# Router products taken from the un-normalised sum in a two-layer decoder trunk

## The reference, cut to what matters

```python
x = layer_norm(DN_ALPHA * x + mix, ln_mix_g[layer], ln_mix_b[layer])
x = layer_norm(DN_ALPHA * x + memory_cross_attention(...), ln_xa_g[layer], ln_xa_b[layer])
x = layer_norm(DN_ALPHA * x + hierarchical_moe(x, ...), ln_ffn_g[layer], ln_ffn_b[layer])

def hierarchical_moe(x, wg, bg, we, be, w1, w3, w2):
    g_logits = xf @ wg + bg                      # 4 groups
    g_star = jnp.argmax(g_logits, axis=-1)
    e_logits = (xf @ we + be)[group g_star]      # 8 experts of the group
    top_val, top_idx = lax.top_k(e_logits, 2)
    ...
    y = (silu(xb @ w1[e]) * (xb @ w3[e])) @ w2[e]   # per expert, weighted and summed
```

## Time and profile before

| what | us |
|---|---|
| median of 3 runs | 1432.13 |
| lowest and highest run | 1429.75, 1433.57 |
| profiled execution, first to last instruction (span) | 1427.2 |
| what the median has beside that span | 4.9 |
| PE busy | 1157.1 (81%) |
| DVE busy | 397.7 (28%) |
| ACT busy | 169.2 (12%) |
| read from memory | 473.62 MB |

### The profile page before, as it was taken

One profiled execution on the slowest core, in us unless ns is written; L12 is line 12 of the kernel. 1 busy time (PEld: TensorE's weight loads), 2 busy tenths in 40 slices (PEclk: granted clock), 3 DMA queues, 4 the chain that ended last, 5 costly groups with the idle time before them and its releaser, 6 DMA issues.

```text
span 1427.2 us, 32903 instructions
## 1 busy us (share of the span) xinstructions
PE 1157.1 (81%) x11774; PEld 723.4 (51%) x11775; DVE 397.7 (28%) x1046; ACT 169.2 (12%) x473; POOL 38.4 (3%) x81
## 2 busy tenths in 40 slices
PE   8999999988797686768789999999987676766665
PEld 7885448554453343334348866655543333333332
DVE  1963532252222121112133123253321111111113
ACT  1202501101110010001010001111110000000001
POOL 4000000001000000000000000000000000000000
PEclk9999999999999898889899999999998888888887
DMA  9756106679999999999995656454999999999994
GB/s 310 269 177 236 60 29 242 266 307 423 429 428 429 428 428 429 428 428 429 428 408 218 236 176 261 163 221 187 410 430 428 428 429 428 429 429 428 428 430 208
DMA packets 64820, 477.34 MB, mean 334 GB/s; under 512 B 4188, under 2 KB 11676, under 8 KB 39948
## 3 DMA queue, kind: packets, MB, share of 16 engines
q1 hardware_dynamic: 62572, 469.97, 80.5%
q0 software_dynamic: 2208, 6.81, 1.5%
HBM read 473.62 MB, written 3.15 MB: 334 GB/s over the span
## 4 chain that ended last, share of the span: by engine, by line
PE 51%; DMA 41%; issue 3%; DVE 2%; ACT 1%; ACTq 1%; SPq 0%; DVEq 0%; POOL 0%
DMA ring<-in_moe_w_dram 41%; PE bank L550 15%; PE bank L959 11%; PE bank L563 8%; PE bank L975 3%; PE bank L744 2%; PE bank L983 2%; PE bank L945 2%; PE bank L520 1%; PE bank L845 1%; PE bank L863 1%; PE bank L902 1%; PE bank L619 1%; PE bank L966 0%; SPq L457 0%
## 5 line engine op out<-in xcount | busy, mean ns | idle before, releaser
L959 PE MATMUL bank<-ring,xT 128*32 128x256 f32 x4672 | 351.0, 466 | 204.4 <-DMA ring<-in_moe_w_dram 200.5
L959 PEld LDWEIGHTS bank<-ring,xT 128*32 128x32 f32 x4672 | 192.3, 133 | 357.9 <-issue 236.1
L550 PE MATMUL bank<-xT,ring 128*128 128x256 f32 x832 | 181.6, 379 | 4.2 <-issue 2.3
L550 PEld LDWEIGHTS bank<-xT,ring 128*128 128x128 f32 x832 | 157.4, 190 | 26.4 <-issue 5.1
L975 PE MATMUL bank<-slot,xT 128*32 128x256 f32 x2336 | 140.1, 380 | 2.7 <-DVE xT L1517 2.5
L1507 DVE SCALAR_TENSOR_TENSOR xT<-xT,bank 64x256 f32<-64x256 f32 x73 | 30.3, 415 | 368.6 <-ACT xT L1750 368.6
L563 PE MATMUL bank<-ring,slot 128*128 128x512 f32 x256 | 111.5, 593 | 4.0 <-ACT slot L1724 2.0
L975 PEld LDWEIGHTS bank<-slot,xT 128*32 128x32 f32 x2336 | 77.4, 110 | 53.9 <-issue 8.7
L983 PE MATMUL bank<-xT 32*128 32x256 f32 x1200 | 85.9, 400 | 19.8 <-issue 18.4
L1493 DVE TENSOR_TENSOR xT<-iota,place 128x64 f32 (+1 forms) x73 | 16.4, 225 | 275.0 <-issue 272.5
L1750 ACT ACTIVATE xT<-bank 64x256 f32<-64x256 f32 x73 | 27.5, 377 | 538.8 <-PE bank L959 520.9
(11 more groups left out here) (273 smaller groups left out, 782.6 us busy)
## 6 DMA issues: line engine op xcount, KB each, us to landing
ring<-in_moe_w_dram SPq DMA_DIRECT2D x126, 2048.0 KB, 33.5
slot<-in_moe_w_dram SPq DMA_DIRECT2D x64, 2048.0 KB, 38.4
ring<-in_od_w_in_dram SPq DMA_DIRECT2D x6, 2048.0 KB, 21.4
ring<-in_xa_wq_dram SPq DMA_DIRECT2D x4, 2048.0 KB, 12.0
ring<-in_xa_wo_dram SPq DMA_DIRECT2D x4, 2048.0 KB, 11.9
ring<-in_ev_w_in_dram SPq DMA_DIRECT2D x3, 2048.0 KB, 14.7
ring<-in_mem_wk_dram SPq DMA_DIRECT2D x2, 2048.0 KB, 15.6
ring<-in_mem_wv_dram SPq DMA_DIRECT2D x2, 2048.0 KB, 12.2
```

The lines of the kernel that those rows point to most:

```text
L550: ins = mm(ps, w[:, k, c0:c0 + P], rhs[:, k, :], start=(k == 4), stop=(k == 3))
L959: ins = mm(b1[qs[2 * m + h], 0:S], xg[:, k, :], ws[m][:, k, h, :, :], start=(k == 0), stop=(k == KC - 1))
```

## The change

In LayerNorm 3L + 1 of both layers, PE no longer waits for the normalised rows. It transposes the sum s = ALPHA * x + f as it stands, and the router's products are taken with s. The logits of LN(s) * gain + bias are

rstd * (s @ (gain * W) - mean * sum(gain * W)) + (bias @ W + router bias),

so W is multiplied by the gain once, at the start of layer 0's mixer projection on DVE (`fold_router`), the sums over features are made by one product with a matrix of ones on PE and taken over by DVE (`take_fold`), and `group_logits` applies mean, rstd and the new bias to 36 columns. The rows of x are made by two instructions of the form (x - mean) * gain and x * rstd + bias (`centred`, `scaled`) where there were three. The transposed rows leave the banks as plain copies. `keep_warm` is gone at this place. Tile 0 and tile 1 are routed one after the other. `start_sum(q, 1)`, q = 1 to 3, is moved behind the hidden layer of the first expert.

```diff
@@ PE
             def normal(i, t):
-                if i % 3 == 2:
+                if i % 3 == 1:
+                    for h in range(2):
+                        wait_drained(pe, ("f", i, t, h))
+                elif i % 3 == 2:
...
             def out_projection(name, i, between=None):
...
                         if t == 1 and h == 0:
                             turned(("n", i), x, 0)
+                            if between is not None:
+                                between()
...
+            def fold_router():
+                ps = claim(pe, ("fold",))
+                pe.wait_ge(wr_folded, 1)
+                n = 2 * DEPTH * (NG + NE)
+                filled(mm(ps[:, 0:n], ones[:, :], scr[:, :, :].rearrange("p a s -> p (a s)")[:, S:S + n], start=True, stop=True), ("fold",))
...
-                out_projection(f"wo_mix{L}", 3 * L)
+                out_projection(f"wo_mix{L}", 3 * L, fold_router if L == 0 else None)
...
-                def logits(t, warm=0):
-                    ps = claim(pe, ("lg", L, t))
-                    keep_warm(ps, warm)
-                    for k in AS_TURNED:
-                        fresh_part(3 * L + 1, k, t)
-                        ins = mm(ps[:, 0:NG + NE], xT[:, k, t * P:(t + 1) * P], wr[:, L, k, :], start=(k == 4), stop=(k == 3))
-                    filled(ins, ("lg", L, t))
-                logits(0)
-                turned(("n", 3 * L + 1), x, 1, 7)
-                logits(1, 6)
+                def logits(t, part):
+                    if part == 0:
+                        claim(pe, ("lg", L, t))
+                        for h in range(2):
+                            wait_drained(pe, (("n", 3 * L + 1), t, h))
+                    ps = banks[bank_of[("lg", L, t)][0]]
+                    for k in range(4 * part, 4 * part + 4):
+                        ins = mm(ps[:, 0:NG + NE], xT[:, k, t * P:(t + 1) * P], wr[:, L, k, :], start=(k == 0), stop=(k == KC - 1))
+                    if part == 1:
+                        filled(ins, ("lg", L, t))
+                if L == 0:
+                    wait_drained(pe, ("fold",))
+                logits(0, 0)
+                turned(("n", 3 * L + 1), x, 1)
+                logits(0, 1)
+                logits(1, 0)
+                logits(1, 1)
...
-                for q in range(1, Q):
-                    start_sum(q, 1)
...
                 unit_hidden(moe_slots[L][0], ready_at(0, 0), 1)
+                for q in range(1, Q):
+                    start_sum(q, 1)
@@ DVE
+        def raw_to_xT(v, i, t):
+            ps = wait_filled(v, (("n", i), t, 1))
+            drained(nc.vector.tensor_copy(xT[:, 4:KC, t * P:(t + 1) * P], ps[:, :].rearrange("p (k s) -> p k s", k=4)), (("n", i), t, 1))
+        def centred(st, v, i, t):
+            v.wait_ge(gb_loaded, 32 * (i + 1))
+            for h in range(2):
+                wait_filled(v, (("n", i), t, h))
+            return st.mark(nc.vector.scalar_tensor_tensor(out=x[:, t, :], in0=x[:, t, :], scalar=mv[:, t, 0:1], in1=gb[:, 0, :],
+                                                          op0=ALU.subtract, op1=ALU.mult))
+        def scaled(st, v, i, t, centred_at):
+            st.wait(centred_at)
+            v.wait_ge(ln_rstd, 2 * i + t + 1)
+            nc.vector.scalar_tensor_tensor(out=x[:, t, :], in0=x[:, t, :], scalar=rstd[:, t, :], in1=gb[:, 1, :],
+                                           op0=ALU.mult, op1=ALU.add).then_inc(x_ready[t], 1)
...
+            def fold_router():
+                v.wait_ge(small_loaded, 16 * 12)
+                flat = scr[:, :, :].rearrange("p a s -> p (a s)")
+                for L in range(DEPTH):
+                    for m in (1, 0):
+                        w = wr[:, L, :, :] if m == 0 else flat[:, 0:KC * NR // 2].rearrange("p (k n) -> p k n", n=NR)
+                        sums = flat[:, S + (2 * L + m) * NR:S + (2 * L + m + 1) * NR]
+                        for half in range(2):
+                            ks = slice(4 * half, 4 * half + 4)
+                            dst = w[:, ks, :] if m == 0 else w
+                            st.do(tt(dst, wr[:, L, ks, :], lngT[:, 3 * L + 1, m, ks].unsqueeze(2).to_broadcast([P, 4, NR]), ALU.mult))
+                            if m == 1:
+                                part = sums if half == 0 else e01[:, :, :, :].rearrange("p t m e -> p (t m e)")[:, 0:NR]
+                                st.do(nc.vector.tensor_reduce(part, w.rearrange("p k n -> p n k"), AX, ALU.add))
+                                if half == 1:
+                                    st.do(tt(sums, sums, part, ALU.add))
+                            elif half == 1:
+                                st.do(nc.vector.tensor_reduce(sums, w.rearrange("p k n -> p n k"), AX, ALU.add))
+            def take_fold():
+                ps = wait_filled(v, ("fold",))
+                v.wait_ge(bias_loaded, 32)
+                for L in range(DEPTH):
+                    ts(wr_sum[:, L, :], ps[:, 2 * L * NR:(2 * L + 1) * NR], -1.0, None, ALU.mult)
+                    ins = tt(rbias[:, L, :], rbias[:, L, :], ps[:, (2 * L + 1) * NR:(2 * L + 2) * NR], ALU.add)
+                drained(ins, ("fold",))
...
                 def group_logits(t):
-                    st.do(tt(g8[:, t, 0:NG], ps[:, 0:NG], rbias[:, L, 0:NG], ALU.add))
-                    drained(tt(lg[:, t, :, :], ps[:, NG:NG + NE].rearrange("p (g e) -> p g e", g=NG),
-                               rbias[:, L, NG:NG + NE].rearrange("p (g e) -> p g e", g=NG), ALU.add), ("lg", L, t))
+                    for dst, c0, c1 in ((groups, 0, NG), (every, NG, NG + NE)):
+                        ins = stt(out=dst, in0=wr_sum[:, L, c0:c1], scalar=mv[:, t, 0:1], in1=ps[:, c0:c1], op0=ALU.mult, op1=ALU.add)
+                        if c0 == 0:
+                            st.mark(ins)
+                    drained(ins, ("lg", L, t))
+                    st.wait()
+                    st.do(stt(out=groups, in0=groups, scalar=rstd[:, t, :], in1=rbias[:, L, 0:NG], op0=ALU.mult, op1=ALU.add))
                     st.do(nc.vector.max(top[:, t, 0, :], g8[:, t, :]))
...
+                    st.do(stt(out=every, in0=every, scalar=rstd[:, t, :], in1=rbias[:, L, NG:NG + NE], op0=ALU.mult, op1=ALU.add))
...
+                i = 3 * L + 1
+                norm_stats(st, v, i, 0, 0)
+                norm_stats(st, v, i, 0, 1)
+                st.wait()
+                row_rstd(v, i, 0, 2)
+                norm_stats(st, v, i, 1, 0)
+                raw_to_xT(v, i, 0)
+                v.wait_ge(ln_stats, 2 * i + 1)
+                scaled(st, v, i, 0, centred(st, v, i, 0))
+                norm_stats(st, v, i, 1, 1)
+                st.wait()
+                row_rstd(v, i, 1, 2)
+                raw_to_xT(v, i, 1)
+                v.wait_ge(ln_stats, 2 * i + 2)
+                at_ = centred(st, v, i, 1)
+                route(0)
+                route(1)
+                scaled(st, v, i, 1, at_)
@@ ACT, norm_act
+                if i % 3 == 1:
+                    drained(nc.scalar.copy(xT[:, 0:4, t * P:(t + 1) * P], ps[:, :].rearrange("p (k s) -> p k s", k=4)), (("n", i), t, 0))
+                    continue
```

More of the change, by code:

```diff
@@ L158, in program @@
         rbias = sb("rbias", [P, DEPTH, NG + NE])
+        wr_sum = sb("wr_sum", [P, DEPTH, NG + NE])
         lg = sb("lg", [P, TT, NG, EPG])
@@ L264, in program @@
         xa_done = sem("xa_done")
+        wr_folded = sem("wr_folded")
         counted = sem("counted")
@@ L505, in normal @@
                 else:
-                    pe.wait_ge(n_ready, 2 * (2 * (i // 3) + i % 3) + t + 1)
+                    pe.wait_ge(n_ready, TT * (i // 3) + t + 1)
             def turned(key, src, t, warm=0):
@@ L533, in fresh_part @@
                 if c < 3:
-                    pe.wait_ge((xT_by_act, xT_by_dve)[h], 3 * (TT * i + t) + c + 1)
+                    pe.wait_ge((xT_by_act, xT_by_dve)[h], 3 * (TT * (i - (i + 1) // 3) + t) + c + 1)
                 else:
@@ L551, in by_weight, with out_projection @@
                 return ins
-            def out_projection(name, i):
+            def out_projection(name, i, between=None):
                 ws = []
@@ L1085, in to_xT, with norm_stats, norm_dve @@
             drained(ins, (("n", i), t, 1))
-        def norm_dve(st, v, i, between=None, behind=None):
+        def norm_stats(st, v, i, t, h):
+            if i and h == 0:
+                v.wait_ge(x_ready[t], i)
+            key = ("f", i, t, h)
+            ps = wait_filled(v, key)
+            xx = x[:, t, h * 512:(h + 1) * 512]
+            drained(nc.vector.scalar_tensor_tensor(out=xx, in0=xx, scalar=ALPHA, in1=ps[:, :], op0=ALU.mult, op1=ALU.add), key)
+            wait_drained(v, key)
+            st.mark(nc.vector.bn_stats(out=bn[:, t, h, :], in_=xx))
+        def norm_dve(st, v, i, behind=None):
             if i == 0:
                 v.wait_ge(small_loaded, 16 * 12)
[L1092 to L1100, removed]
             def plain(t):
@@ L1106, in plain @@
```

(57 more changed lines are left out.)

1 line of the change is left out of this document (removed).

## The result

| kernel | median us (runs) | ratio to the kernel before, 95% interval |
|---|---|---|
| before | 1432.01 (20) | |
| changed | 1434.78 (20) | 1.0017 [1.0009, 1.0025] |

The change costs 0.17%, 2.4 us by the ratio; the forecast was 1432.6 with a range of 1429.0 to 1436.5 and no difference beyond 0.3% as the likeliest outcome. The measured median lies in the range. The profiled execution of the changed kernel has a span of 1433.0 us and took 1434.77; the profile of before (1427.2) is of one of its shorter executions, so these two spans can't be compared with each other.

What follows compares the result with a forecast made beforehand. Transfers were taken to bound the expert loops, PE the rest, DVE the seam between; -1.1 + 0 + 0.3 = -0.8, plus 1.3 for one clock fall, gave a span of 1427.7, with 4.9 to the median 1432.6 us, range 1429.0 to 1436.5.

Steps and rivals of the forecast that it cites:

- DVE seam: From last residual sum to first hidden layer: taking a wait from PE gains only what it takes from DVE's stream.
- DVE's steps: DVE's stream in the seam: copy 0.69, `centred` 1.22, routing 3.05 a tile, `scaled` of tile 1 starting at 10.45.
- `centred` and `scaled` at half rate: Rival, chance 0.05: the two row instructions take 2.44 each; sum +3.6, 1435.7 us.
- -0.3 in each layer: Seam of each layer: DVE takes up positions at 303.1 instead of 303.42.
- Moved sums: Residual products behind the first hidden layer: layer 0's first two transfers restart 1.4 earlier, following ones gain less.
- -1.1 in layer 0: Gain in layer 0's expert loop; at most 0.3 + 0.9 = 1.2, less if a later issue has less in hand.
- 0 between +0.5 and -0.3: Moved residual products in layer 1: gain 0.5 if PE's pause of 0.78 fits under them, otherwise 0.3 lost; taken as 0.
- Fold: Mixer projection: 18 DVE steps, about 5.5 us, inside a pause of 10.67; one unhidden PE product costs +0.3.
- PE's clock: Seam: a new PE pause of 2.5 before zeros and residual products lets the clock fall in one of the two layers.
- 1.3 a time: Price of one clock fall: 2.75 of PE's work behind the pause slowed, taken between bounds of 0 and 2.75.
- -0.8 + 1.3 = +0.5: Whole kernel: -0.8 without a clock effect plus 1.3 for one clock fall, added to the profiled span of 1427.2.
- slower by the clock: Rival, chance 0.25: the clock falls in both layers, +1.8, 1433.9 us; extreme case +6.8, 1438.9.

Runs made afterwards that it cites:

- a filled pause: The changed kernel with 11 products on zeros in PE's pause between the router's last product and the claim of the result banks, both layers; ratio to before 0.9968.
- warm_sums_back: The changed kernel with PE's pause filled by products on zeros and the moved residual products back in front of the first hidden layer; ratio to before 0.9976.
- sums_back: The changed kernel with residual products q = 1 to 3 of tile 1 back before the first hidden layer, PE's pause left unfilled; ratio to before 1.0026.
- other_bank: The changed kernel with the router's bank of tile 1 outside the four result banks, so PE's pause comes behind the residual products; ratio to before 0.9992.
- warm_layer0: The changed kernel with PE's pause filled by 11 products on zeros in layer 0 alone; ratio to before 1.0006.
- warm_layer1: The changed kernel with PE's pause filled by 11 products on zeros in layer 1 alone; ratio to before 0.9998.
- the loop filled too: The changed kernel with PE's pause filled and, in layer 0, eight more products on zeros ahead of the expert loop; ratio to before 0.9976.
- warm_five: The changed kernel with five products on zeros, not eleven, in PE's pause in both layers; ratio to before 0.9978.
- before_no_warm: The kernel before with keep_warm (7 and 6 products on zeros) taken out of the router's place alone; ratio to before 1.0067.

## Why the prediction was right, and where a term was off

*DVE seam.* Right. In all changed kernels with PE at full clock up to there the positions come at 11.2 to 11.3, whatever PE does in between.

*DVE's steps.* Right in kind, 0.45 too long up to the take-up of positions. Forecast was a start of `scaled` at 10.45, measured 10.1: routing takes 2.95 instead of 3.05 a tile, and the copy comes 0.1 earlier; the rest lies behind `scaled`. `centred`, 1.28, was priced at 1.22. Twice the time of the one-operation row, 2.44, did not show, so what the Trainium skill says of this form ("Vector Engine (DVE) Microarchitecture Reference", section "Points that are easy to get wrong") is not confirmed here against that row, and the rival `centred` and `scaled` at half rate is out. Positions at full clock come 0.8 earlier than before, not 0.3: **-0.3 in each layer** was too small by 0.5.

*Moved sums.* The hidden layer starts earlier, the third transfer much less, as forecast. The first issue gained 1.8 with a filled pause (17.43 against 19.22), the third 0.6 (27.55 against 28.18). So **-1.1 in layer 0** was too large: 0.6 at this place. A gap between second and third transfer was what I had named as a sign of error, and it is there even with a filled pause: a DMA share of 0.84 from 322 to 324 (0.57 in the second half), with the issues 10.1 apart (forecast 10, before 9.0). What was in hand was used up. In layer 1 I had taken 0 between +0.5 and -0.3. With a filled pause the restart comes at 26.44 instead of 27.70. 0.9 of it is there with the sums in their old place (26.78 in warm_sums_back), 0.3 comes by the sums; the kernel before gains 0.4 by them alone (27.29). So PE's pause did fit under them, in part.

*Fold.* 6.3 us on DVE instead of 5.5 (for 16 steps, not 18), covered. PE's product takes 0.41, and from the third mixer sum to the fourth there are 7.99 us instead of 210.64 - 202.88 = 7.76: +0.2 for the +0.3.

*PE's clock: the mis-sized term.* The pause was forecast at 2.5 and is 2.4 to 2.6. That the clock would fall was right; that it would do so in one layer of two was not: in the eight seams of this study with an unfilled pause of 2.4 to 2.6 (changed kernel 2, sums_back 2, other_bank 2, one each in warm_layer0 and warm_layer1) it fell in the pause or, in the two of other_bank, within 2.5 us behind it. The price was **1.3 a time**; the profile shows 2.36 in layer 0 (13.66 against 11.30) and 1.94 in layer 1 (13.12 against 11.18), and the ratios 5.6 to 7.0 for both. Both errors have the same sign, and the gain that I had underrated has the other. That the sum came near is luck: forecast -0.8 + 1.3 = +0.5, measured +2.4, made of -3 to -4.6 at full clock and 5 to 7 for two falls. The case that came in was the rival "slower by the clock", with a chance of 0.25, whose 1433.9 was closer than the forecast.

Open is why the kernel with a filled pause is 3 to 4.6 us faster than before, by the ratios of five kernels with overlapping intervals (0.9968 to 0.9980), when places in the seams account for some 1.7 (0.6 in layer 0, 1.3 in layer 1, less 0.2 for the fold). From layer 0's last sum to the end, the single profiles have 1135.8 us before and 1134.4 to 1135.3 in four of the five kernels (1132.8 with the loop filled too), which is 0.5 to 1.4 less; another 0.2 is in the time outside of the span (2.0 before, 1.8 in the changed kernels). The rest would lie ahead of the seam, where the last sum of layer 0 starts between 290.3 and 294.9, in no order that goes with the kernels. The times of single executions of one kernel scatter by 4 to 11 us, and the clock's falls elsewhere differ from one to the next (around 752 and 875 in the changed kernel's profile, neither in that of before), so single profiles can't tell it.

## What to carry to other kernels

When a wait is taken from an engine that isn't the bound, look at what it does with the time. Here PE's wait for rows became a longer wait for a bank, the filler products were deleted with it, and a pause of 2.5 us made the following 2.75 us of PE's work take 5.0 to 5.3, just where that work leads. Count filler products as part of the schedule: five of them in each layer turned a loss of 0.17% into a gain of 0.2%.

## What was unexpected of the hardware

Pauses of 1.50 and 1.35 us, behind filler products, left the granted clock at 1.00 in both seams of warm_five; pauses of 2.4 to 2.6 were followed by 0.50 in eight of eight, and in the kernel before 2.58 before 332.36 was not the earlier trace rows. The length of a pause alone doesn't tell: in before_no_warm, the clock fell in both layers in a pause of 1.84 that stands right behind router products (1.95) with no filler, stayed at 0.50 for most of the seam, and the kernel lost 0.67%.
